# A decoder block in fp32: the first norm's scale row moved from the rows into the raw in-projection weights

## The chip, the cores and the metric

The kernel runs on one core of a Trainium2 chip. A core has TensorE (PE, matmuls; its weight loads are PEld), VectorE (DVE), ScalarE (ACT), GpSimd (POOL) and SyncE (SP, here used only to issue DMAs). They run side by side and are kept in order by semaphores. The metric is the device time of one execution in microseconds; less is better.

## The reference

One layer, 1024 tokens, 1024 channels, all float32:

```
h    = rms_norm(x, norm_mix_pre)              # x * rsqrt(mean(x*x) + eps) * gain
proj = h @ w_in                               # 1024 -> 1792 columns
y    = concat(pool_mixer, conv_mixer, sliding-window attention with sinks)
x    = x + rms_norm(y @ w_o, norm_mix_post)
h    = rms_norm(x, norm_ffn_pre)
up   = causal_dwconv(h @ ffn_w_up) + b        # gate and value, 2816 each
x    = x + rms_norm((silu(gate) * value) @ ffn_w_down, norm_ffn_post)
```

The change concerns the first two lines only. The gain `norm_mix_pre` has one number for each of the 1024 input channels, so (x * r * gain) @ w_in is the same as (x * r) @ (gain * w_in) with the gain on the rows of w_in.

## The kernel before

Tokens lie in eight tiles of 128, channels in eight blocks of 128 (KD), the 1792 in-projection columns in fourteen weight tiles of 128 columns (`IN_ORDER` gives their order). A float32 product is made of three fp32r matmuls: each operand is split into a high part, rounded by ScalarE (`whi`, `hhi`), and a low part, the difference, made by VectorE (`wlo`, `hlo`). TensorE multiplies high by high, high by low and low by high (`product`, lines 1616 to 1618).

The opening works as follows. SP loads x tiles into `xin` (three places, used in turn), the identity matrix, the first gain as eight rows of 128 (`gain_rows`), and again broadcast over all partitions (`gain_a`), and the raw weights into `wraw` (four places, used in turn; a place is loaded again when the low part of its tile is made). For each x tile ScalarE sums the squares (`square_x`), GpSimd makes the reciprocal root (`root`), VectorE writes the normed rows into `hrow_a` (`norm_x`, two places), TensorE turns them so that channels lie on partitions (`turn_x`, eight transposes into two PSUM banks), ScalarE rounds the result to `hhi` (`round_h`) and VectorE makes `hlo` (`low_h`).

Tiles 0 and 1 are normed without the gain, because the broadcast row is not there yet. TensorE transposes `gain_rows` so that the gain lies on channel partitions (line 1684), VectorE copies that to `gain_t`, and multiplies both turned tiles by it in PSUM (`scale_turned`, line 1155). Tiles 2 to 7 are multiplied by root and gain in one instruction (line 1131).

TensorE projects weight tiles 0 and 1 first, two x tiles (a pair) at a time, as the pairs become ready. For pair 0 the products are made pass by pass (`channels_by_pass`, line 1664: eight matmuls for a pass, three passes for a weight tile), with the turns of tiles 2 and 3 between passes; for pairs 1 to 3 in the usual order of `product`. Ahead of the first product TensorE multiplies zeros to keep its clock (`keep_clock`). Weight tiles 2 to 13 follow, with all eight x tiles there; from tile 5 on they are interleaved with the attention's sixteen units (scores, mask, exponentials, `norm_probs`, `turn_probs`, products with the values). Weight tile n is rounded by `round_ring(n)` on ScalarE and `low_ring(n)` on VectorE.

GpSimd's order in this part is: the eight roots, four small DMAs of the pool weights, three small memsets, four DMAs that copy blocks of `w_down` in DRAM, a wait until they are done, two DMAs that add further blocks, a wait, one more, and then the roots of the second norm. Each engine's instructions run in the order in which they are written.

## Time and profile before

| what | value |
|---|---|
| time, median of 3 runs | 950.21 us (949.88 to 950.55) |
| span of the profiled execution, first to last instruction | 948.2 us |
| the median of the runs, beyond that span | 2.0 us |
| TensorE busy | 938.9 us (99%) |
| VectorE busy | 654.7 us (69%) |
| ScalarE busy | 433.5 us (46%) |
| GpSimd busy | 189.4 us (20%) |
| mean granted TensorE clock | 0.999 of 2.4 GHz |

The page of a profile gives each engine's busy time, and the chain of waits: the work that ended last, followed back from the end, each step to what released it. The timeline lists instructions with start and duration; times in it are microseconds from the start of the span.

### The profile page before, as it was taken

Reading aid. Unit: us, or ns where it says so; the run is one execution under the profiler, and the core shown is the slowest. Engines: PE = TensorE matmul, PEld = TensorE weight load, DVE = VectorE, ACT = ScalarE, POOL = GpSimd, SP = SyncE. Lnnn points to the kernel's source line nnn. Section 1 sums busy time; section 2 is a strip of 40 time slices with the busy share of each in tenths; the row PEclk is TensorE's granted clock in tenths of the full one; section 3 lists DMA queues with packets and bytes.
Section 4 is the critical chain, followed back from the end, with each engine's and each line's share of the span. In section 5 each row is a group of like instructions: output and inputs, shape, how many; then the busy total and the mean of one; then the engine's idle time right before and its main releaser. Section 6 shows DMA issues by size and latency. Waiting matters only on the chain.

```text
span 948.2 us, 11487 instructions
## 1 busy us (share of the span) xinstructions
PE 938.9 (99%) x4419; PEld 777.9 (82%) x4419; DVE 654.7 (69%) x710; ACT 433.5 (46%) x648; POOL 189.4 (20%) x182
## 2 busy tenths in 40 slices
PE   8999999999999999999999999999999999999997
PEld 7988887887888888888888888888888888888886
DVE  6645795766655899777877787778776653535668
ACT  5524444444433555445443444444444454335353
POOL 3301000000111424242223333443431100000021
PEclk9999999999999999999999999999999999999999
DMA  6999971005322236486343446554647775677455
GB/s 225 269 328 231 209 145 45 23 23 178 134 89 89 90 97 206 142 184 183 115 141 100 145 112 133 112 143 105 140 91 208 201 235 214 228 267 264 163 171 200
DMA packets 114248, 151.16 MB, mean 159 GB/s; under 512 B 6289, under 2 KB 66193, under 8 KB 114193
## 3 DMA queue, kind: packets, MB, share of 16 engines
q1 hardware_dynamic: 100737, 118.63, 38.5%
q0 software_dynamic: 13456, 31.79, 16.8%
q8 instruction: 35, 0.57, 0.3%
q14 instruction: 20, 0.16, 0.1%
HBM read 113.17 MB, written 60.29 MB: 183 GB/s over the span
## 4 chain that ended last, share of the span: by engine, by line
PE 97%; DVE 1%; DMA 0%; ACT 0%; POOL 0%; issue 0%; DVEq 0%; POOLq 0%; SPq 0%; ACTq 0%
PE ps L1616 30%; PE ps L1618 30%; PE ps L1617 30%; PE ps L1626 1%; PE ps L1751 1%; PE ps L1774 1%; PE ps L1752 1%; PE ps L1760 1%; PE ps L1778 1%; DMA xin<-in_x 0%; DVE hlo L1138 0%; PE ps L1789 0%; DVE ps L1155 0%; PE ps L1664 0%; DVE x2b L1427 0%
## 5 line engine op out<-in xcount | busy, mean ns | idle before, releaser
L1616 PE MATMUL ps<-hhi,whi 128*128 128x512 f32 (+1 forms) x240 | 91.1, 379 | 0.5 <-DVE hlo L1138 0.5
L1618 PE MATMUL ps<-hhi,wlo 128*128 128x512 f32 (+1 forms) x240 | 88.5, 369 | 0.0
L1617 PE MATMUL ps<-hlo,whi 128*128 128x512 f32 (+1 forms) x240 | 88.5, 369 | 0.0
L686 POOL TENSOR_TENSOR w_sums<-wraw 128x1024 f32<-128x1024 f32 x20 | 48.4, 2421 | 185.8 <-DVE w2lo L1373 63.0
L648 POOL TENSOR_SCALAR meansq<-sumsq 128x1 f32<-128x1 f32 x28 | 10.0, 357 | 373.4 <-ACT yg L1042 170.8
L1616 PEld LDWEIGHTS ps<-hhi,whi 128*128 128x128 f32 x240 | 45.3, 189 | 8.0 <-DVE hlo L1138 0.7
L1001 ACT ACTIVATE yg<-ps,par_b 128x1024 f32<-128x1024 f32 x21 | 25.3, 1207 | 57.9 <-DVE ps L1499 57.9
L1618 PEld LDWEIGHTS ps<-hhi,wlo 128*128 128x128 f32 x240 | 45.2, 189 | 7.7
L1617 PEld LDWEIGHTS ps<-hlo,whi 128*128 128x128 f32 x240 | 45.3, 189 | 7.4 <-issue 0.5
L1447 DVE SCALAR_TENSOR_TENSOR yg<-ps,par_a,yg 128x1023 f32<-128x1023 f32 x22 | 28.2, 1282 | 26.9 <-ACT yg L1001 26.9
L1616 PE MATMUL ps<-h2hi,whi 128*128 128x512 f32 x116 | 45.4, 391 | 0.2 <-DVE wraw L1148 0.2
L1618 PE MATMUL ps<-h2hi,wlo 128*128 128x512 f32 x116 | 45.2, 389 | 0.0
L1617 PE MATMUL ps<-h2lo,whi 128*128 128x512 f32 x116 | 45.1, 389 | 0.0
L1461 DVE TENSOR_TENSOR w2lo<-wraw,w2hi 128x1024 fp32r<-128x1024 f32 x23 | 27.8, 1223 | 23.5 <-ACT w2hi L1031 23.1
L1616 PE MATMUL ps<-r_hi,whi 128*128 128x512 f32 x112 | 43.6, 389 | 0.0
L1618 PE MATMUL ps<-r_hi,wlo 128*128 128x512 f32 x112 | 43.6, 389 | 0.0
L1618 PE MATMUL ps<-r_hi,w2lo 128*128 128x512 f32 x112 | 43.6, 389 | 0.0
L1616 PE MATMUL ps<-r_hi,w2hi 128*128 128x512 f32 x112 | 43.6, 389 | 0.0
L1617 PE MATMUL ps<-r_lo,w2hi 128*128 128x512 f32 x112 | 43.6, 389 | 0.0
L1616 PE MATMUL ps<-r_hi,h2hi 128*128 128x512 f32 x112 | 43.6, 389 | 0.0
L1617 PE MATMUL ps<-r_lo,h2hi 128*128 128x512 f32 x112 | 43.6, 389 | 0.0
L1618 PE MATMUL ps<-r_hi,h2lo 128*128 128x512 f32 x112 | 43.6, 389 | 0.0
(261 smaller groups left out, 2709.1 us busy)
## 6 DMA issues: line engine op xcount, KB each, us to landing
wraw<-in_ffn_w_up SPq DMA_DIRECT2D x42, 512.0 KB, 5.2
s_dram<-in_ffn_w_down POOLq DMA_DIRECT2D x6, 2816.0 KB, 28.1
wraw<-r_dram SPq DMA_DIRECT2D x44, 256.0 KB, 3.7
wraw<-s_dram SPq DMA_DIRECT2D x44, 256.0 KB, 4.9
r_dram<-cst SPq DMA_DIRECT2D x33, 256.0 KB, 2.8
wraw<-act_dram SPq DMA_DIRECT2D x33, 256.0 KB, 3.6
wraw<-in_ffn_w_down SPq DMA_DIRECT2D x33, 256.0 KB, 4.6
wraw<-in_w_in SPq DMA_DIRECT2D x14, 512.0 KB, 10.2
```

The costliest lines, as they stand in the source:

```text
L648: pool.tensor_scalar(meansq[:, i:i + 1], sumsq[:, i:i + 1], 1.0 / DM, EPS, ALU.mult, ALU.add).then_inc(ms_ready, 1)
L686: pool.tensor_tensor(w_sums[:, 0:2, :], raw[:, 0:4:3, :], raw[:, 2:3, :].broadcast_to([P, 2, HALF]), ALU.add)\
L1001: act.activation(yg[:, pair % 2, :], banks(4 * (pair % 2)), ACT.Identity, bias=ffn_bias(pair), scale=ffn_tap(2, pair)).then_inc(yg_started, 1)
L1447: finish_step(dve.scalar_tensor_tensor(y[:, 1:], src[:, :SEQ - 1], ffn_tap(1, f), y[:, 1:], ALU.mult, ALU.add))
L1461: dve.tensor_tensor(lo, raw, hi, ALU.subtract).then_inc(d_split, 1)
L1616: pe.matmul(acc, w_hi, x_hi, start=first, stop=False, skip_group_check=looped)
L1617: pe.matmul(acc, w_hi, x_lo, start=False, stop=False, skip_group_check=looped)
L1618: return pe.matmul(acc, w_lo, x_hi, start=False, stop=last, skip_group_check=looped)
L1626: last = pe.transpose(ps[:, b + k // 4, (k % 4) * P:(k % 4 + 1) * P], rows[:, k * P:(k + 1) * P], ident)
L1751: pe.matmul(acc, q, k_hi[:, kv, keys], start=True, stop=False)
L1752: last = pe.matmul(acc, q, k_lo[:, kv, keys], start=False, stop=True)
L1760: last = pe.transpose(ps[:, 6, i * P:(i + 1) * P], s_sb[:, u % 2, i, :], ident)
```

## The change

The gain is no longer multiplied into rows or turned tiles. It is multiplied into the raw weights in `wraw` before these are split. Weight tile 0: the first half on GpSimd (`times_gain`), the second half on VectorE. Weight tile 1: not in place; ScalarE rounds it in eight pieces of 128 columns with the gain as the activation's scale (`round_second`), and VectorE makes the low part in eight pieces (`low_second`). Weight tiles 2 to 13: GpSimd, one instruction each, put between its roots and DMA issues.

Every x tile gets its own place in `xin` and is normed in place, so the loads of x wait for nothing; the squares go to a scratch tile. `hhi` of tile 1 is copied from PSUM by VectorE instead of ScalarE. The broadcast load of the first gain is dropped; the load of the second norm's gain into `gain_a` no longer waits for the rows. The order of SP's loads changes, as do the orders on ScalarE and VectorE for tiles 2 and 3, the places of the turns of tiles 2 and 3 among TensorE's passes, and the split of the keep-clock matmuls.

```
+        gain_t = half_sums
-        xin = alloc(xa, "xin", [P, 3, DM])
-        hrow_a = alloc(xa, "hrow_a", [P, 2, DM])
-        gain_t = alloc(xa, "gain_t", [P, KD])
+        xin = alloc(xa, "xin", [P, NT, DM])
+        squares = alloc(xa, "squares", [P, DM])
...
+        def over_channels(ks):
+            return gain_t[:, ks].rearrange("p (k o) -> p k o", o=1)\
+                .broadcast_to([P, ks.stop - ks.start, P])
...
 SP
             def load_x(t):
-                if t >= 3:
-                    sp.wait_ge(hrow_ready, t - 2)
-                sp.dma_start(xin[:, t % 3, :], x_d[t * P:(t + 1) * P, :])\
-                  .then_inc(xin_in[t % 3], 16)
+                sp.dma_start(xin[:, t, :], x_d[t * P:(t + 1) * P, :]).then_inc(xin_in[t], 16)
             load_x(0)
-            load_x(1)
             sp.dma_start(cst[:, 0:P], consts[:, 0:P]).then_inc(ident_in, 16)
             sp.dma_start(gain_rows[0:KD, :], norm_mix_pre[0].rearrange("(k p) -> k p", p=P))\
               .then_inc(gain_rows_in, 16)
+            load_x(1)
             load_in(0)
             load_x(2)
             load_x(3)
-            sp.dma_start(gain_a[:, :], norm_mix_pre.broadcast_to([P, DM])).then_inc(gain_in, 16)
             load_in(1)
...
-            for n in range(RAW, 6):
+            for n in range(RAW, 7):
                 load_in(n)
-            sp.wait_ge(hrow_ready, NT)
             sp.dma_start(gain_a[:, :], norm_mix_post.broadcast_to([P, DM]))\
               .then_inc(gains_mix_in, 16)
...
 GpSimd
+            def times_gain(n, ks=slice(0, KD)):
+                pool.wait_ge(landed[n % RAW], 16 * (n // RAW + 1))
+                pool.wait_ge(gain_taken, 1)
+                raw = wraw[:, n % RAW, :].rearrange("p (k c) -> p k c", k=KD)[:, ks, :]
+                pool.tensor_tensor(raw, raw, over_channels(ks), ALU.mult).then_inc(gained, 1)
-            for i in range(NT):
+            root(0, 1)
+            root(1, 2)
+            times_gain(0, slice(0, KD // 2))
+            for i in range(2, NT):
                 root(i, i + 1)
+            times_gain(2)
+            times_gain(3)
...          (four DMAs of pool_w)
+            times_gain(4)
+            times_gain(5)
...          (memsets, four DMAs that copy w_down blocks)
+            for n in range(6, 10):
+                times_gain(n)
...          (two DMAs that add blocks)
+            times_gain(10)
+            times_gain(11)
...          (one DMA that adds)
+            times_gain(12)
+            times_gain(13)
 ScalarE
+            def round_second():
+                act.wait_ge(landed[1], 16)
+                act.wait_ge(gain_taken, 1)
+                for k in range(KD):
+                    w = slice(k * P, (k + 1) * P)
+                    last = act.activation(whi[:, 1, w], wraw[:, 1, w], ACT.Copy,
+                                          scale=gain_t[:, k:k + 1])
+                last.then_inc(w_rounded, 1)
             square_x(0)
             square_x(1)
+            round_h(0, hhi)
             round_ring(0)
-            round_h(0, hhi)
-            round_h(1, hhi)
             square_x(2)
             square_x(3)
-            round_ring(1)
-            for t in range(2, NT, 2):
+            round_h(2, hhi)
+            round_second()
+            round_h(3, hhi)
...          (then squares and rounding by pairs, as before)
 VectorE
+            def low_second():
+                dve.wait_ge(w_rounded, 2)
+                for k in range(KD):
+                    w = slice(k * P, (k + 1) * P)
+                    last = dve.scalar_tensor_tensor(wlo[:, 1, w], wraw[:, 1, w], gain_t[:, k:k + 1],
+                                                    whi[:, 1, w], ALU.mult, ALU.subtract)
+                last.then_inc(w_split, 1)
+            dve.wait_ge(gain_turned, 1)
+            dve.tensor_copy(gain_t[:, :], ps[:, 3, 0:KD]).then_inc(gain_taken, 1)
             norm_x(0)
             norm_x(1)
-            dve.wait_ge(gain_turned, 1)
-            finish_step(dve.tensor_copy(gain_t[:, :], ps[:, 3, 0:KD]))
-            scale_turned(0)
-            scale_turned(1)
+            dve.wait_ge(landed[0], 16)
+            dve.wait_ge(gain_taken, 1)
+            raw_late = wraw[:, 0, DM // 2:].rearrange("p (k c) -> p k c", k=KD // 2)
+            dve.tensor_tensor(raw_late, raw_late, over_channels(slice(KD // 2, KD)), ALU.mult)\
+               .then_inc(gained_late, 1)
+            dve.wait_ge(turned, 2)
+            dve.tensor_copy(hhi[:, 1, :, :].rearrange("p k c -> p (k c)"), banks(*turn_banks(1)))\
+               .then_inc(ht_rounded, 1)
             low_ring(0)
             low_h(0, hhi, hlo)
+            norm_x(2)
             low_h(1, hhi, hlo)
-            norm_x(2)
             norm_x(3)
-            low_ring(1)
+            low_h(2, hhi, hlo)
+            low_second()
+            low_h(3, hhi, hlo)
...          (then norms and low parts by pairs, as before)
 TensorE
-                    if n == 1 and i < 2:
-                        turn_x(2 + i)
+                    if n == 0 and i == 2:
+                        turn_x(2)
+                    if n == 1 and i == 0:
+                        turn_x(3)
...
-            keep_clock(8)
+            keep_clock(6)
...          (the gain's transpose)
+            keep_clock(3)
             turn_x(0)
             turn_x(1)
-            keep_clock(4)
+            keep_clock(3)
```

## Rows read from the trace of the kernel before

**Rows 1.** Busy time by stretch: stretch, its length, then each engine's busy time (instructions).

```profile
0.00:12.20 12.20, 9.64 (x41) 7.55 (x41) 5.01 (x7) 6.70 (x9) 2.38 (x11) 1.00 0.82 263
...
21.10:200.00 178.90, 178.78 (x1002) 149.16 (x1003) 117.47 (x193) 78.65 (x209) 15.17 (x22) 1.00 0.67 169
200.00:948.00 748.00, 742.30 (x3314) 613.62 (x3312) 523.93 (x505) 341.66 (x424) 169.29 (x145) 1.00 0.52 155
```

**Rows 2.** Chain of waits up to 21.5 us: start, duration, what.

```profile
1.17 4.40 DMA xin<-in_x
...
7.91 0.49 DVE hrow_a L1126
...
8.77 2.36 DVE ps L1155 x2
...
12.26 2.28 DVE hlo L1138 x2
...
15.86 1.06 PE ps L1626 x8
16.93 0.96 PE ps L1664 x8
...
19.86 1.24 DVE hlo L1138
21.14 0.39 PE ps L1616
```

**Rows 3.** Groups of 0 to 220 us (busy, mean ns), then timeline rows of SP, ScalarE and TensorE.

```profile
L1116 DVE TENSOR_TENSOR wlo<-wraw,whi 128x1024 fp32r<-128x1024 f32 x14 | 17.1, 1220 | 4.4 <-ACT whi L744 4.3
L1126 DVE TENSOR_SCALAR hrow_a<-xin,rstd 128x1024 f32<-128x1024 f32 x2 | 1.5, 754 | 7.2 <-POOL rstd L651 7.2
L1255 DVE TENSOR_TENSOR s_sb<-s_sb,small 128x512 f32<-128x512 f32 x16 | 11.1, 692 | 0.5
...
1.64 0.42 SPq L550 DMA_DIRECT2D cst<-consts_dram  x1
...
8.30 1.06 ACT L744 ACTIVATE whi<-wraw 128x1024 fp32r<-128x1024 f32 x1 [1.55 <-DMA wraw<-in_w_in]
...
15.30 1.06 ACT L744 ACTIVATE whi<-wraw 128x1024 fp32r<-128x1024 f32 x1 [1.03 <-DMA wraw<-in_w_in]
...
12.24 1.21 PE L1664 MATMUL ps<-hhi,whi 128*128 128x256 f32 x8 [0.70 <-ACT hhi L768]
```

**Rows 4.** L686 and L693 alone (duration min/median/max), then timeline of GpSimd and VectorE.

```profile
L686 POOL TENSOR_TENSOR w_sums<-wraw x20: 2384/2391/2702, 341.0 to 689.4; 128x1024 f32<-128x1024 f32 x20
L693 POOL TENSOR_TENSOR w_sums<-w_sums,wraw x20: 1292/1292/1297, 346.9 to 693.5; 128x512 f32<-128x512 f32 x20
...
317.11 4.34 POOL L686 TENSOR_TENSOR w_sums<-w_second 128x1024 f32<-128x1024 f32 x1 [1.45 <-DVE hrow_c L1439]
...
316.89 2.28 DVE L1377 TENSOR_TENSOR r_lo<-wraw,r_hi 128x2048 fp32r<-128x2048 f32 x1
...
324.70 3.38 DVE L1385 SCALAR_TENSOR_TENSOR wraw<-wraw,h2hi 128x2048 f32<-128x2048 f32 x1
```

**Rows 5.** Timeline of ScalarE: one exponential of 128 columns and what follows it.

```profile
80.58 0.39 ACT L825 ACTIVATE s_sb<-s_sb,small 128x128 f32<-128x128 f32 x1
80.87 0.19 ACT L825 ACTIVATION_READ_ACCUMULATOR s_sb<-s_sb,small 128x1 f32 x1
```

**Rows 6.** Timeline: GpSimd's last root, VectorE's low part of weight 2, its first matmul.

```profile
30.76 0.55 POOL L651 TENSOR_TENSOR rstd<-meansq,power 128x1 f32<-128x1 f32 x1
...
40.72 1.23 DVE L1116 TENSOR_TENSOR wlo<-wraw,whi 128x1024 fp32r<-128x1024 f32 x1 [4.34 <-ACT whi L744]
...
42.42 0.48 PE L1616 MATMUL ps<-hhi,whi 128*128 128x512 f32 x1
```

**Rows 7.** Timeline of VectorE and TensorE: unit 2's probabilities normed, and their turn.

```profile
97.14 0.69 DVE L1255 TENSOR_TENSOR s_sb<-s_sb,small 128x512 f32<-128x512 f32 x1
...
98.79 0.62 PE L1760 MATMUL ps<-cst,s_sb 128*128 128x128 f32 x4
```

More of the change, by code:

```diff
@@ L259, in build @@
         gain_turned = sem("gain_pre_on_channel_partitions")
-        scaled = sem("first_turned_rows_scaled")
+        gain_taken = sem("gain_pre_taken_from_psum")
+        gained = sem("weights_times_gain_pre")
+        gained_late = sem("second_half_of_first_weights_times_gain_pre")
         consts_in = sem("consts_in")
@@ L263, in build @@
         pool_w_in = sem("pool_w_in")
-        gain_in = sem("gain_pre_in")
         gains_mix_in = sem("gains_mix_in")
         gain_out_in = sem("gain_out_in")
-        xin_in = [sem(f"xin_in{i}") for i in range(3)]
+        xin_in = [sem(f"xin_in{i}") for i in range(NT)]
         xres_in = sem("xres_in")
@@ L573, in _ @@
             sp.dma_start(sinks[:, :], attn_sinks.broadcast_to([P, NH])).then_inc(params_in, 16)
-            for n in range(RAW, 6):
+            for n in range(RAW, 7):
                 load_in(n)
-            sp.wait_ge(hrow_ready, NT)
             sp.dma_start(gain_a[:, :], norm_mix_post.broadcast_to([P, DM]))\
               .then_inc(gains_mix_in, 16)
-            for n in range(6, NIN):
+            for n in range(7, NIN):
                 load_in(n)
@@ L742, in round_weight @@
                 n = base + RAW * q
-                act.wait_ge(landed[base % RAW], 16 * (base // RAW + 1 + q))
+                if n == 0:
+                    act.wait_ge(gained, 1)
+                    act.wait_ge(gained_late, 1)
+                elif n < NIN:
+                    act.wait_ge(gained, n)
+                else:
+                    act.wait_ge(landed[base % RAW], 16 * (base // RAW + 1 + q))
                 act.activation(hi[:, slot, :], wraw[:, base % RAW, :], ACT.Copy)\
@@ L751, in round_ring @@
                 round_weight(n, 0, whi, r % SPLIT)
+            def round_second():
[6 more added lines that the diff above has]
+                last.then_inc(w_rounded, 1)
             def square_x(t):
-                act.wait_ge(xin_in[t % 3], 16 * (t // 3 + 1))
-                if t >= 2:
-                    act.wait_ge(turned, t - 1)
-                act.activation(hrow_a[:, t % 2, :], xin[:, t % 3, :], ACT.Square,
+                act.wait_ge(xin_in[t], 16)
+                if t:
+                    act.wait_ge(squared, t)
+                act.activation(squares[:, :], xin[:, t, :], ACT.Square,
                                accum_out=sumsq[:, t:t + 1]).then_inc(squared, 1)
             def round_h(i, hi):
-                if i < 2:
-                    act.wait_ge(scaled, i + 1)
                 act.wait_ge(turned, i + 1)
@@ L772, in _ @@
             square_x(1)
+            round_h(0, hhi)
             round_ring(0)
-            round_h(0, hhi)
-            round_h(1, hhi)
             square_x(2)
             square_x(3)
-            round_ring(1)
-            for t in range(2, NT, 2):
+            round_h(2, hhi)
+            round_second()
+            round_h(3, hhi)
+            for t in range(4, NT, 2):
+                square_x(t)
+                square_x(t + 1)
                 round_h(t, hhi)
                 round_h(t + 1, hhi)
-                if t + 2 < NT:
-                    square_x(t + 2)
-                    square_x(t + 3)
             def take(m):
@@ L1632, in turn_x @@
                     pe.wait_ge(ht_split, t - 1)
-                turn(t, hrow_a[:, t % 2, :])
+                turn(t, xin[:, t, :])
             def channels(acc_bank, slot, hi, lo, tiles, ks=range(KD)):
```

28 lines of the change are left out of this document (8 added, 20 removed).

## The prediction

> **What bounds the kernel now.** I read the busy time by stretch first. From 21.1 us to 200 us TensorE is busy 178.78 of 178.90 us, and from 200 us to the end 742.3 of 748; the first 12.2 us hold 2.56 us without TensorE work [rows 1]. DMA is busy about two thirds of the time behind 21.1 us, ScalarE and VectorE less. So TensorE's own work is the bound, the change alters none of the products, and it can win only what lies ahead of the first ordinary matmul of tile pair 1, which starts at 21.14 us. Everything behind follows that start, since TensorE has no gap in which a later start could be made up. The change can lose in two places: in this opening, and wherever GpSimd's new work makes VectorE late for TensorE further on.
>
> The chain of waits tells what the opening is made of [rows 2]: x tile 1 lands at 5.57; its squares and root, and its norm at 7.91; both turned tiles times the gain on VectorE, 2.36 us; wlo; two hlo to 14.54; then passes of eight matmuls on TensorE with the turns of tiles 2 (15.86) and 3 between them, a last hlo of tile 3 (19.86), and pair 1 at 21.14. From 8.77 to 14.54 VectorE alone sets the pace.
>
> **The change, part by part.** Durations are in [rows 3]; consecutive VectorE and ScalarE instructions overlap by about 0.1 us.
>
> *Removed.* The two products L1155 (2.36 us on the chain). The product into rows of tiles 2 to 7 becomes the plain scaling that tiles 0 and 1 have now, 0.75 us (L1126). The gain broadcast and the waits of the x loads leave SP's early queue; that hides nothing from the bound, because from x tile 1 on no transfer stands in the chain. Weight tile 1 comes earlier than now, when ScalarE waited for it until 15.30; that matters only if ScalarE is free for it, and below it is not.
>
> *x tile 1 later.* The identity (64 KB) and the gain rows (4 KB) now go ahead of it. Tile 1 took 4.40 us from issue to landing behind tile 0's 512 KB [rows 2]; 68 KB at the 263 GB/s of this stretch [rows 1] is 0.26 us. If the later issue counts instead, it is two issues of 0.42 us, 0.9 with what lies between. I take the bytes, since tile 0 keeps the DMA engines at work meanwhile: tile 1 lands at 5.8, and the norm starts between 8.05 and 8.15 instead of 7.91; I go on with 8.05. With the norm's 0.75 us and the turn's 1.1 (L1626 in rows 2) the turned tile is there at 9.95.
>
> *The gain into weight tile 0.* Weight tile 0 lands at about 8.3 as before (ScalarE's rounding waited for it until 8.30), as the bytes ahead of it are the same. Then half of it is multiplied on GpSimd and half on VectorE. GpSimd: 1.29 us for 128x512 (L693). VectorE: 0.69 us (L1255, the same shape with a broadcast small operand). They are meant to run side by side. The trace speaks against that [rows 4]: GpSimd's L686 takes 2.39 us as a rule and 4.34 us when VectorE's L1377, with both inputs in SBUF, was under way (316.89 to 319.17); 319.17 plus 2.39 is 321.56, and it ended at 321.45. The other way round, VectorE's L1385 took 3.38 us, 1.1 more than L1377 took for as many elements, while GpSimd was at work on the last sum of the same tile. One waits for the other to end. The same at 8 us: the norm of tile 1 runs 8.05 to 8.8, GpSimd's half 8.8 to 10.1, VectorE's half 10.1 to 10.8, ScalarE's rounding of whi 10.8 to 11.85. Without the waiting GpSimd would be done at 9.6, and the first product would start at 11.3 (behind the copy of the turned tile 1, 10.0 to 11.25), 0.65 us earlier than with it.
>
> The Trainium skill has this rule ("SBUF — State Buffer", Who interferes with whom): a VectorE instruction with two SBUF inputs contends with a GpSimd instruction that reads SBUF, and the one that starts first keeps the port to its end. The rows above agree. By the rule the opening ends 0.65 us later than if both halves ran in parallel; the sum takes the rows' value, which is the same.
>
> *hhi of tile 1 on VectorE.* 1.2 us like L1116, behind VectorE's half of the gain: 10.75 to 11.95. First product at 11.95 instead of 12.24 [rows 3]. Then VectorE does wlo (11.9 to 13.1), hlo of tile 0 (to 14.25), the norm of tile 2 (to 14.9), hlo of tile 1 (to 16.05). Before, the two hlo ended at 14.54.
>
> *Tiles 2 and 3 and weight tile 1.* The turn of tile 2 starts at 14.95 instead of 15.86; with 1.1 us for the turn ScalarE rounds tile 2 from 16.05 to 17.1. Now comes the dear part: weight tile 1 is rounded in eight pieces of 128 columns with a per-partition scale, where one instruction of 1.06 us did it. The nearest row is L825, the same shape: 0.39 us, and 0.29 us from one start to the next instruction's [rows 5]. Eight make 2.4 us (bounds: 8 x 0.2 = 1.6, the 0.19 us of an instruction with one element, and 8 x 0.39 = 3.1). ScalarE: 17.0 to 19.4. Before, whi of tile 1 was ready at 16.36. VectorE's wlo in eight pieces: between 128x512 (0.69) and 128x1024 (1.22) an element costs 1.03 ns and an instruction 0.16, so a piece is 0.30, with the overlap 0.21, together 1.7 us instead of 1.22: 19.4 to 21.1. hlo of tile 3 follows, 21.05 to 22.3. TensorE: third pass of weight 0 from 16.1, turn of tile 3 to 18.0, wait, weight 1's three passes 19.4 to 22.3 (0.96 us each, the pass of 16.93 in rows 2). Pair 1 starts at 22.35 instead of 21.14: **plus 1.2 us**. Bounds: pieces at 1.6 us and no waiting between GpSimd and VectorE give 20.9 (minus 0.2); the longer pieces and x tile 1 at 0.9 us late give 23.8 (plus 2.7).
>
> *Keep-clock matmuls* move (6, 3, 3 instead of 8 and 4) and cost nothing: they lie in waits, and the later three end at about 11.2, ahead of 11.95.
>
> *GpSimd's twelve other tiles.* Twelve of 128x1024 at 2.39 us are 28.7 us on an engine that is busy 15.2 of 178.9 us [rows 1], so none is on the path by itself. A tile's place is loaded again three weight tiles ahead of its use, 144 matmuls at a mean of 0.18 us or 26 us, and one product takes 2.39. Moved behind them are GpSimd's own DMA issues: the copies of the w_down blocks start 8 to 10 us later (four products), their sums too; they are read in the last stage only, and the transfers of weights 7 to 13 beside them stay as crowded as now. What counts is whom a product blocks. First, GpSimd's last root was done at 31.31 [rows 6], now 1.2 later; the norm of tile 7 (0.75), weights 2 and 3 (4.8) and four DMA issues (0.4 to 0.6 each) put weights 4 and 5 at about 40.3 to 45. VectorE's low part of weight 2, before at 40.72, ends 0.47 us ahead of its user. Shifted by 1.2 it comes at 41.9, is held until 42.7 and ends at 43.9 where TensorE wants it at 43.6: **plus 0.3** (bounds 0 and 2.0). Second, in the attention stage the normed probabilities of unit 2 are ready 0.96 us ahead of TensorE's turn of them [rows 7], and in eight others of the sixteen units 1.1 to 1.4 us; a product that starts just before a VectorE instruction with two SBUF inputs holds it up to 2.39 us. Weights 9 to 13 come here as they land, about one in two units. Most overlaps stay within the spare time; I take one that goes 0.2 us beyond it: **plus 0.2** (bounds 0 and 5 x 1.4 = 7).
>
> *SP.* The x tiles and weights 1 to 3 are issued one behind the other (12 issues of 0.42 us, by 7 us); the load of the second norm's gain goes behind weight 6 and is wanted behind the attention. Nothing.
>
> Sum: 1.2 + 0.3 + 0.2 = 1.7 us on a span of 948.2. The median of the runs is 950.21, 2.0 above the span; I add the sum to it: **951.9 us**. A measurement tells about 0.2% (1.9 us) from no change, so this is within it, on the slow side.
>
> **The rivals.**
> 1. *The opening is nearly even.* If the pieces are cheap or the two halves do run side by side, pair 1 starts between 20.9 and 21.7: 950.0 to 950.9. For: an activation of 128 columns needs little of its 0.39 us for the columns. Against: [rows 4, 5].
> 2. *Slower: GpSimd's products hold VectorE in the attention stage.* Place: weights 9 to 13, on the chain from a unit's scores to its normed probabilities. Spare is about 1.1 us; a full block is 2.39. It decides the sign as soon as blocks beyond the spare add up to 0.5 us more than I took. With three of five hit at a mean 0.65 over the spare it is 2.0 instead of 0.2: 953.7. For: VectorE is busy 117 of 179 us there, and low parts and probabilities all have two SBUF inputs. Against: the tiles land at times that TensorE's order doesn't choose, and some units have 3 us to spare.
> 3. *The clock.* TensorE now waits about 1.4 us ahead of weight 1 and 0.9 us ahead of tile 2's turn. Granted clock stays 1.00 over 2.56 us of waits now [rows 1]. Should it fall to 1.2 GHz for 3 us of work, they take 3 more: 954.9.
> 4. *Faster: the whole of L1155 is won.* If ScalarE's and VectorE's pieces hide behind TensorE, pair 1 starts at 21.14 - 2.36 + 0.15 = 18.9, minus 2.2: 948.0. It needs weight 1's high part by 16.5, before the turn of tile 3 is over; ScalarE would have to take the pieces ahead of tile 2, and its order doesn't.
>
> **How the numbers follow.** Forecast 0.45 (own range 950.5 to 953.0, two thirds of it within 0.2%), rival 1 0.20, rival 2 0.22, rival 3 0.05, rival 4 0.08. Faster by over 0.2% (below 948.3): 0.08. Slower (above 952.1): 0.15 + 0.22 + 0.05 = 0.42. Within: 0.50. The range leaves out rival 4, rival 3 and the far end of rival 2: 949.6 to 954.2.
>
> **What the profile after will show.** First product near 11.95; GpSimd's half of weight 0 at 1.3 us but starting to count only when the norm of tile 1 is over, or VectorE's half far longer than 0.69 us; eight activations over about 2.4 us from 17; TensorE idle ahead of weight 1's first pass; pair 1 at 22.35. VectorE's low part of weight 2 longer than 1.22 us. In the attention stage idle TensorE time where there was none, each with a GpSimd product beside it. I am wrong if pair 1 starts before 20.9 or after 23.8, or if GpSimd and VectorE show their usual durations side by side.

## The result, and the profile after

The changed kernel takes **960.00 us** (median of 4 runs, 959.37 to 961.88) against 950.22 us (949.88 to 950.55): ratio 1.0106, interval 1.0094 to 1.0118. It is slower by 9.8 us. The prediction was 951.9 us with a range of 949.6 to 954.2: wrong, and by far more than its range. The profiled executions stand 10.3 us apart (958.5 against 948.2 us).

Busy time by stretch of the changed kernel, read as in [rows 1] (stretch, length, busy time of TensorE, weight loads, VectorE, ScalarE, GpSimd, granted clock, DMA share, GB/s):

```profile
0.00:12.20 12.20, 7.77 (x31) 6.16 (x32) 3.04 (x4) 4.68 (x7) 3.17 (x12) 0.95 0.83 267
12.20:21.10 8.90, 8.10 (x52) 7.13 (x50) 7.17 (x7) 5.38 (x11) 1.63 (x4) 0.87 1.08 357
21.10:200.00 178.90, 172.82 (x968) 144.07 (x969) 123.73 (x189) 77.73 (x202) 37.27 (x34) 1.00 0.63 157
200.00:958.00 758.00, 752.57 (x3371) 621.93 (x3369) 530.18 (x518) 345.93 (x437) 169.78 (x145) 1.00 0.52 153
```

Between 21.1 and 200 us TensorE had 0.12 us without work before; now it has 6.08. Behind 200 us it idles 5.4 us of 758 against 5.7 of 748, so nothing is lost there. Of the 6.08, 1.18 us belong to a wait of the opening (ahead of 22.28). Two places carry the loss: the opening and the attention stage.

**The opening.** The chain of waits of the changed kernel up to the passes of weight 1:

```profile
2.05 5.63 DMA xin<-in_x
...
7.70 1.16 ACT squares L794 x2
...
9.79 1.53 DVE xin L1169
...
11.37 1.98 PE ps L1663 x8
...
13.37 1.23 DVE hhi L1198
14.60 1.13 DVE wlo L1151
15.73 1.14 DVE hlo L1175
16.86 0.67 DVE xin L1169
...
17.67 1.08 PE ps L1663 x8
...
22.28 3.35 PE ps L1703 x24
```

Timeline rows of the same kernel that belong to it (start, duration, instruction, idle time before it and what ended it):

```profile
9.73 1.04 POOL L660 TENSOR_TENSOR wraw<-wraw,half_sums 128x512 f32<-128x512 f32 x1
...
11.37 1.97 PE L1663 MATMUL ps<-cst,xin 128*128 128x128 f32 x8 [3.17 <-DVE xin L1169]
...
25.54 0.39 PE L1653 MATMUL ps<-hhi,whi 128*128 128x256 f32 x1
```

And two microseconds of the turn of tile 1, as stretches (the third figure from the right is the granted clock):

```profile
12.00:13.00 1.00, 1.00 (x7) 1.00 (x6) 0.00 (x0) 0.99 (x2) 0.00 (x0) 0.50 1.07 356
13.00:14.00 1.00, 1.00 (x5) 0.82 (x4) 0.63 (x1) 1.00 (x3) 0.00 (x0) 0.50 1.03 401
```

These rows show four things. x tile 1 lands at 7.68 us, not at 5.57 [rows 2]. Its norm takes 1.53 us instead of 0.75: GpSimd's half of weight 0 started at 9.73, 0.06 us ahead of it. TensorE has nothing to do for 3.17 us and comes back at the lower of its two clock levels (0.50, that is 1.2 GHz), so that the turn takes 1.97 us instead of 1.1. Pair 1 starts at 25.54 instead of 21.14: **4.4 us**, where the prediction had 1.2.

**From there to 44 us.** The norm of the last x tile is held in the same way by the gain of weight 2, and TensorE waits 0.42 us for it. These are the timeline rows of GpSimd's root of that tile, its products, VectorE's norm, and TensorE's turn:

```profile
34.40 0.55 POOL L652 TENSOR_TENSOR rstd<-meansq,power 128x1 f32<-128x1 f32 x1
34.91 4.20 POOL L660 TENSOR_TENSOR wraw<-wraw,half_sums 128x1024 f32<-128x1024 f32 x2
...
34.98 2.38 DVE L1169 TENSOR_SCALAR xin<-xin,rstd 128x1024 f32<-128x1024 f32 x1 [0.71 <-POOL rstd L652]
...
37.50 1.06 PE L1663 MATMUL ps<-cst,xin 128*128 128x128 f32 x8 [0.42 <-DVE xin L1169]
```

**The attention stage.** One stretch of the timeline shows it: rows of VectorE, of GpSimd, and TensorE's turn of the probabilities:

```profile
94.02 2.14 DVE L1292 TENSOR_TENSOR s_sb<-s_sb,small 128x512 f32<-128x512 f32 x1
96.08 0.73 DVE L1276 COPY_PREDICATED s_sb<-cst,ps 128x512 f32<-128x512 uint32 x1
96.85 0.69 DVE L1280 TENSOR_REDUCE small<-s_sb 128x4 f32<-128x512 f32 x1
97.57 3.00 DVE L1281 SCALAR_TENSOR_TENSOR small<-small,neg_sinks 128x4 f32<-128x4 f32 x1
...
91.85 3.75 POOL L660 TENSOR_TENSOR wraw<-wraw,half_sums 128x1024 f32<-128x1024 f32 x2 [4.06 <-DMA wraw<-in_w_in]
95.55 1.54 POOL L685 DMA_DIRECT2D s_dram<-in_ffn_w_down  x1
96.45 2.16 POOL L687 DMA_DIRECT2D s_dram<-in_ffn_w_down  x1
97.33 3.20 POOL L660 TENSOR_TENSOR wraw<-wraw,half_sums 128x1024 f32<-128x1024 f32 x1
...
96.21 0.66 PE L1800 MATMUL ps<-cst,s_sb 128*128 128x128 f32 x4 [1.03 <-DVE s_sb L1292]
```

The probabilities' product with two inputs in SBUF, 0.69 us before [rows 3], takes 2.14 while GpSimd works on weights 8 and 9. An instruction of 128x4, 0.16 to 0.17 us elsewhere, takes 3.00. The two between them take their usual time; they have one SBUF input and start beside the DMA issues alone. (In e12, below, the same two start inside a product, at 87.92 and 88.70, and take 0.74 and 0.69 us as well. One SBUF input is no safeguard for every instruction, though: the norm of the rows has one, beside a number for each partition, and it was held above.) TensorE's idle time behind 44 us is 4.5 us, in waits of 1.03, 0.74, 1.20 and 1.38 us that VectorE ends and some smaller ones; its granted clock is 1.00 there throughout. GpSimd's root of the second norm, a mark behind the attention, comes at 244.44 instead of 234.15. So 10.3 us = 4.4 (pair 1) + 0.3 (from there to the first matmul of weight 2, at 47.15 instead of 42.42) + 5.6. The 1.1 us by which the 5.6 exceed the idle time come in steps of 0.1 to 0.3 us around the waits; what makes them stays open.

### The profile page after: what moved, and what is told of

It reads as the page before. It is cut to its first block, busy times and chain, and to the rows that moved or that the text cites. A ratio compares the mean times of both kernels' runs of the same rounds, so it can differ in the third digit from the quotient of the medians.

```text
span 958.5 us, 11525 instructions
## 1 busy us (share of the span) xinstructions
PE 941.3 (98%) x4419; PEld 779.3 (81%) x4419; DVE 664.1 (69%) x717; ACT 433.7 (45%) x654; POOL 211.9 (22%) x195
## 4 chain that ended last, share of the span: by engine, by line
PE 89%; DVE 7%; ACT 2%; issue 1%; DMA 1%; POOL 0%; SPq 0%; DVEq 0%; POOLq 0%; ACTq 0%
PE ps L1653 28%; PE ps L1655 28%; PE ps L1654 28%; PE ps L1663 1%; DVE wlo L1151 1%; DVE pool_d L1331 1%; DVE s_sb L1292 1%; DVE s_sb L1276 1%; DMA xin<-in_x 1%; DVE small L1280 1%; ACT s_sb L860 1%; PE ps L1814 1%; PE ps L1791 1%; DVE q_parts L1244 1%; DVE xin L1169 0%
## 5 line engine op out<-in xcount | busy, mean ns | idle before, releaser
L660 POOL TENSOR_TENSOR wraw<-wraw,half_sums 128x1024 f32<-128x1024 f32 (+1 forms) x13 | 26.1, 2021 | 80.5 <-DMA wraw<-in_w_in 80.5
L1654 PE MATMUL ps<-r_lo,whi 128*128 128x512 f32 x112 | 43.6, 389 | 0.0
## 6 DMA issues: line engine op xcount, KB each, us to landing
wraw<-in_w_in SPq DMA_DIRECT2D x14, 512.0 KB, 13.8
```

The costliest lines, as they stand in the source:

```text
L660: pool.tensor_tensor(raw, raw, over_channels(ks), ALU.mult).then_inc(gained, 1)
L1654: pe.matmul(acc, w_hi, x_lo, start=False, stop=False, skip_group_check=looped)
```

## The experiments

Results, all in microseconds; "pair 1" is the start of the first ordinary matmul in the profiled execution (21.14 before, 25.54 after). The runs e3, e5, e6, e10 and e11 leave part of the gain out, so they compute something else and only tell what the rest costs. Each run has one trace. With x tile 1 issued second it landed between 5.57 and 5.86 us in seven of them (before, e1, e5, e6, e9, e10, e11); in its later place it landed at 6.82, 7.07, 7.23, 7.68 and 8.09 (e12, e3, e4, after, e2). Differences of a microsecond between single traces of the later place can therefore be scatter. The kernel before had medians of 950.30 (e1 to e4), 950.36 (e5 to e8) and 950.19 (e9 to e12) beside them.

| run | median (range) | ratio to before, interval | pair 1 |
|---|---|---|---|
| e1 x tile 1 second | 961.39 (959.94–963.17) | 1.0118 (1.0103–1.0133) | 22.56 |
| e2 weight 0 all on VectorE | 961.55 (956.85–962.91) | 1.0110 (1.0084–1.0136) | 24.64 |
| e3 no gain in weights 2 to 13 | 952.92 (952.29–953.57) | 1.0028 (1.0018–1.0038) | 24.06 |
| e4 before, x tile 1 late | 951.28 (950.78–952.29) | 1.0011 (1.0001–1.0020) | 22.57 |
| e5 e1 and e3 together | 951.35 (950.90–951.98) | 1.0011 (1.0001–1.0020) | 23.27 |
| e6 e1 without weight 10's gain | 958.09 (957.25–959.54) | 1.0083 (1.0069–1.0096) | 22.62 |
| e7 e4, x tile 1 transferred alone | 951.17 (950.69–951.77) | 1.0009 (1.0000–1.0018) | 22.25 |
| e8 before, gain spread by TensorE | 952.32 (950.49–952.89) | 1.0014 (1.0005–1.0023) | 22.06 |
| e9 e1, weights 2 to 13 by pieces | 955.28 (954.38–957.14) | 1.0050 (1.0034–1.0065) | 23.78 |
| e10 e5, weight 0 all on VectorE | 950.92 (950.27–951.61) | 1.0007 (0.9999–1.0016) | 22.13 |
| e11 e5, x loads wait again | 951.31 (951.14–951.66) | 1.0013 (1.0004–1.0021) | 22.78 |
| e12 after, clock kept | 957.37 (956.41–961.77) | 1.0084 (1.0064–1.0104) | 24.30 |

**e1: x tile 1 second again.** In the changed kernel:

```
             load_x(0)
+            load_x(1)
             sp.dma_start(cst[:, 0:P], consts[:, 0:P])...
             sp.dma_start(gain_rows[0:KD, :], ...)...
-            load_x(1)
```

> The changed kernel with one difference: SP issues x tile 1 directly behind x tile 0 again, ahead of the identity and the gain rows. Theory A (the place in SP's order makes x tile 1 late, and that lateness makes TensorE wait long enough to lose its clock): tile 1 lands near 5.6 us instead of 7.7, TensorE's granted clock stays at 1.00 in the opening, the first product starts at 12 to 12.5 us instead of 14.9, pair 1 at about 22.5 instead of 25.5, and the time is 956.5 to 957.5 us. Rival B (tile 1 is late because the loads of x and of the weights, now issued without waits, share the DMA engines): it still lands after 7 us and the time stays at 959.5 or more.

The opening came out nearly as the prediction had drawn it: the norm started at 8.10, the halves of weight 0 ran one behind the other, the clock stayed at 1.00, pair 1 started at 22.56 (predicted 22.35). That is 3.0 us earlier than after, and yet the time didn't fall: Theory A had the opening right and the time (956.5 to 957.5) wrong. The attention stage lost what the opening had won. Timeline rows of e1 on VectorE, GpSimd and TensorE:

```profile
92.02 5.10 DVE L1292 TENSOR_TENSOR s_sb<-s_sb,small 128x512 f32<-128x512 f32 x1
...
91.58 1.54 POOL L685 DMA_DIRECT2D s_dram<-in_ffn_w_down  x1
92.48 2.16 POOL L687 DMA_DIRECT2D s_dram<-in_ffn_w_down  x1
93.36 3.20 POOL L660 TENSOR_TENSOR wraw<-wraw,half_sums 128x1024 f32<-128x1024 f32 x1
...
97.17 1.12 PE L1800 MATMUL ps<-cst,s_sb 128*128 128x128 f32 x4 [4.94 <-DVE s_sb L1292]
```

And its stretches from inside that wait on:

```profile
95.00:100.00 5.00, 2.83 (x9) 2.44 (x10) 4.90 (x7) 1.84 (x7) 1.56 (x1) 0.50 1.07 178
100.00:105.00 5.00, 5.00 (x20) 3.93 (x19) 4.69 (x7) 0.66 (x5) 0.00 (x0) 0.86 1.12 204
```

One instruction of 0.69 us was held for 5.10, TensorE waited 4.94, and its clock fell to 0.50 within that wait and stayed there until 101.4. From 97.2 to 101.4 TensorE worked at half speed, which is some 2.1 us lost (an estimate from these two times). Where the products land against VectorE's work decides, and here they met a worse place than in the changed kernel.

**e2: the gain of weight 0 on VectorE alone**, the GpSimd half taken out of the changed kernel:

```
-            times_gain(0, slice(0, KD // 2))
-            raw_late = wraw[:, 0, DM // 2:]...          (four channel blocks)
+            raw_late = wraw[:, 0, :]...                 (all eight)
```

> The changed kernel with one difference: all of weight tile 0 is multiplied by the gain on VectorE, in one instruction of 128x1024, and nothing of it on GpSimd. Theory A (GpSimd's half took the shared port first and held the norm of x tile 1 from 0.75 to 1.52 us): the norm of tile 1 takes 0.75 us, its turn starts 0.75 us earlier and the time falls by 0.7 to 1.2 us (less waiting, perhaps less of the low clock), to about 959. Rival (the two engines' halves do save time together, since the product on VectorE alone is 1.22 instead of 0.68 us): the first product starts no earlier, and the time is 960 or more.

The norm of tile 1 took its 0.75 us again (it started at 10.21, as x tile 1 landed at 8.09), and pair 1 started at 24.64, 0.9 earlier than after. The clock fell to 0.50 all the same, at 11.9, behind a wait of 2.50 us. The time tells nothing: its runs lie 6 us apart, and the profiled one has a wait of 5.2 us in the attention stage. The hold of the norm is shown by the trace, its price in the time is not.

**e3: no gain in weights 2 to 13**, all twelve GpSimd products out of the changed kernel:

```
-            times_gain(2)
...
-            times_gain(13)
```

> The changed kernel without the gain in weight tiles 2 to 13 (this part of the computation is left out; the opening with weight tiles 0 and 1 is unchanged): GpSimd has none of its twelve products and ScalarE rounds as the tiles land. Theory A (GpSimd's products hold VectorE's instructions with two SBUF inputs, and that is all of the loss between 44 and 200 us): TensorE has no waits there, and the time is 5.0 to 5.6 us below the changed kernel, about 954.6. Rival (the loss there comes from the new order of loads and of the w_down copies, or from late weights): at least 2 us of waits stay in that stretch, and the time is above 956.5.

Windows of e3, same columns:

```profile
25.00:40.00 15.00, 15.00 (x130) 15.00 (x129) 6.98 (x7) 6.07 (x8) 5.42 (x13) 1.00 0.11 29
40.00:80.00 40.00, 40.00 (x207) 34.25 (x207) 16.61 (x17) 13.16 (x14) 2.74 (x4) 1.00 0.98 312
...
80.00:200.00 120.00, 120.00 (x653) 96.85 (x652) 88.80 (x163) 57.93 (x184) 4.55 (x3) 1.00 0.59 122
```

TensorE has no gap left behind 25 us, and the time falls by 7.1 us (960.00 to 952.92). In the profiled executions 1.5 of that stand in the opening, where no product of these differs (x tile 1 landed at 7.07 instead of 7.68), so the twelve products are worth some 5.6 to 7.1 us. The remaining 2.6 us over before are the opening. The rival (late weights, the new order of loads) is out: the orders are the same here and no wait is left. There is a second sign. In the traces without the twelve products (before, e3, e5, e9) no VectorE instruction between 21 and 210 us takes over 0.12 us more than the shortest of its kind; in the changed kernel seven do, by 11.7 us in all, and each overlaps a product.

**e4: the kernel before, with x tile 1 issued behind the identity and the gain rows**, as in the change:

```
             load_x(0)
-            load_x(1)
             sp.dma_start(cst[:, 0:P], consts[:, 0:P])...
             sp.dma_start(gain_rows[0:KD, :], ...)...
+            load_x(1)
```

> The kernel before with one difference: the identity and the gain rows are issued ahead of x tile 1, as in the changed kernel; x tile 3 still waits for the first normed row. Theory A (place in the order alone): tile 1 lands at 7.0 to 7.7 us instead of 5.57, the opening is later by 1.5 to 3 us, time 951.7 to 953.2. Rival B (only together with the x loads that no longer wait): tile 1 lands by 6.2, time within 0.7 us of 950.2. The estimate of the prediction was 5.8 us.

The time rose by 1.0 us, less than the 1.5 that Theory A gave at the least, though the landing is the one it gave. x tile 1 was issued 0.88 us later (2.05 against 1.17) and landed 1.66 us later (7.23 against 5.57).

**e7: why it lands so late.** e4, with SP waiting for x tile 1 before it issues weight 0:

```
             load_x(1)
+            sp.wait_ge(xin_in[1], 16)
             load_in(0)
```

> The kernel before with the identity and the gain rows issued ahead of x tile 1, and SP waiting until tile 1 has landed before it issues weight tile 0. Theory A (tile 1 lands 1.7 to 2.1 us late because its packets share the DMA engines with those of weight tile 0 and x tile 2, once it has lost its lead): it lands at 5.5 to 6.1 us here, while weight tile 0 comes late and sets the opening (time about 951.5 to 953). Rival (the small transfers ahead of it, the identity in 512 byte pieces and the gain rows, cost it that time themselves): it lands at 7.0 or later.

x tile 1 from issue to landing in the chain of waits of e4:

```profile
2.05 5.18 DMA xin<-in_x
```

The same of e7:

```profile
2.05 4.27 DMA xin<-in_x
```

Alone it takes 4.27 us and lands at 6.32. So of the 1.66 us, 0.9 goes with the traffic issued behind it and 0.8 with the two small loads ahead. That is a split of single traces; the 6.32 lies below all five landings of the later place (6.82 to 8.09), so the direction is safe and the sizes are rough. In the kernel before it took 4.40 [rows 2], hardly longer than alone. That it was well under way there when the next loads came is my explanation, which no run tests. Neither expectation of e7 held alone.

**e5: x tile 1 second and no gain in weights 2 to 13** (the edits of e1 and e3).

> The changed kernel with x tile 1 issued directly behind tile 0 and without the gain in weight tiles 2 to 13 (that part of the computation is left out): GpSimd has only its half of weight tile 0. What is left of the change is its opening. Theory A (the losses add up: late x tile 1 with the low clock about 3 us, GpSimd's later products the rest): pair 1 starts near 22.6 us as in the run with tile 1 second, no TensorE waits behind it, time 951.5 to 952.0 us, which is what the prediction gave for the opening alone (plus 1.2, and 0.3). Rival (another loss stays behind 21 us): 953 or more.

951.35 us, where 951.5 to 952.0 were expected, and no wait of TensorE behind the opening; pair 1 came at 23.27 instead of 22.6. Against e1, which differs by the twelve products alone, that is 10.0 us. With the pair after and e3 (7.1) this gives their price twice, and shows that it depends on where they land. Counted from pair 1 on in the traces, the prices are 8.8 and 6.2 us. The runs with tile 1 second show another thing. In e1, e5, e9 and e11 weight tile 0 landed between 8.79 and 10.01, it heads the chain of waits, and pair 1 starts 13.8 us behind it each time. In e6 and e10 it landed at 8.70 and 8.23, and VectorE's own chain was about as late (13.9 us). So once tile 1 is early, the transfer of weight tile 0 can set the opening; the prediction had it at 8.3 and off the chain.

**e6: e1 without weight 10's gain alone**, the product that stands behind two DMA issues.

```
-            times_gain(10)
```

> The changed kernel with x tile 1 second and without the product of weight tile 10 alone (its gain is left out), the one that stands behind GpSimd's two issues of the w_down sums and held a 0.69 us instruction of VectorE for 5.10 us. Theory A (the large loss is that pile: product 8 and 9, two DMA issues, product 10 back to back, and the low clock that follows the long wait): the wait of 4.9 us near 92 us falls under 1.5 us, the clock stays at 1.00 and the time falls by 4 to 6 us, from about 961 to 955 to 957. Rival (each of the twelve products costs about the same, 0.5 to 0.8 us): the time falls by less than 1.5 us.

3.3 us less than e1, a third of the 10.0, so the other eleven cost twice as much together, if the prices add up. Theory A (4 to 6 us) gave too much and the rival (under 1.5) too little. The wait near 92 us fell to 2.06 us, not under 1.5, and the clock still fell to 0.50 there (94.8 to 98.2). Timeline of e6, VectorE and GpSimd:

```profile
90.92 0.98 DVE L1287 TENSOR_TENSOR small<-small 128x4 f32<-128x4 f32 x1 [1.22 <-ACT small L862]
...
92.15 2.14 DVE L1291 TENSOR_TENSOR s_sb<-s_sb,small 128x512 f32<-128x512 f32 x1
...
95.70 0.16 DVE L1280 SCALAR_TENSOR_TENSOR small<-small,neg_sinks 128x4 f32<-128x4 f32 x1
...
93.68 1.54 POOL L685 DMA_DIRECT2D s_dram<-in_ffn_w_down  x1
94.58 2.16 POOL L687 DMA_DIRECT2D s_dram<-in_ffn_w_down  x1
```

Products 8 and 9 still hold two instructions (0.98 and 2.14 us). The DMA issues alone hold none: 0.16 us at 95.70, in their midst, and the traces without products show the same. It takes a product behind them to hold VectorE, and then, in e1, from 92.02, before the product's own record begins at 93.36.

**e9: the gain of weights 2 to 13 without GpSimd**, by eight pieces each on ScalarE and VectorE, as weight 1 has it (with e1's order of loads; the whole computation is done):

```
+                if 2 <= n < NIN:           (round_ring; low_ring has the same)
+                    for k in range(KD):
+                        w = slice(k * P, (k + 1) * P)
+                        last = act.activation(hi[:, slot, w], wraw[:, base % RAW, w], ACT.Copy,
+                                              scale=gain_t[:, k:k + 1])
```

> The changed kernel with x tile 1 second and GpSimd's products of weight tiles 2 to 13 replaced: these tiles take the gain as tile 1 does, in eight scaled pieces on ScalarE and eight on VectorE (the whole computation is there). Each tile costs ScalarE 2.4 instead of 1.06 us and VectorE 2.2 instead of 1.22, in the order in which they worked before, and nothing holds the shared port. Theory A (what the twelve products cost, 10.0 us in the versions with tile 1 second, is the port and not the work): 951.4 to 953 us, waits of TensorE behind 21 us under 1.5 us in all. Rival (VectorE and ScalarE have no room in the attention stage for any more work): above 955.

955.28 us. With the products off GpSimd no VectorE instruction is held between 21 and 210 us, and 6.1 of e1's 10.0 us come back; the other 3.9 (over e5) are the price of the pieces. The time is what the rival gave (above 955), but the want of room is not in the attention stage: of 2.4 us that TensorE idles between 44 and 210 us, 1.8 stand ahead of weight 2 (first row below) and 0.6 in the attention stage. The clock was at 0.50 from 47.6 to 51.0, behind that wait. The profiled run is the slowest of the four (957.14). Timeline of e9, where TensorE waits for a low part in pieces:

```profile
46.82 0.47 PE L1656 MATMUL ps<-hhi,whi 128*128 128x512 f32 x1 [1.82 <-DVE wlo L1149]
...
52.32 2.19 DVE L1149 SCALAR_TENSOR_TENSOR wlo<-wraw,half_sums,whi 128x128 fp32r<-128x128 f32 x8
```

**e10: e5 with the gain of weight 0 on VectorE alone** (the edit of e2).

> As the run with x tile 1 second and no gain in tiles 2 to 13, and with all of weight tile 0 multiplied on VectorE (one 128x1024 product) instead of half on each engine. If the two halves run one after the other (1.29 and 0.69 us, 2.0 together with the wait), VectorE alone with 1.22 us brings whi of tile 0 some 0.3 to 0.6 us earlier, and the time falls from 951.35 to 950.7 to 951.1. If they run side by side as the change has it, it rises by 0.5.

950.92 us, 0.4 less than e5, or 0.3 when each is compared with the kernel before beside it. Timeline rows, of e10's VectorE and of e5's GpSimd:

```profile
8.70 1.22 DVE L1181 TENSOR_TENSOR wraw<-wraw,half_sums 128x1024 f32<-128x1024 f32 x1
...
9.57 1.54 POOL L660 TENSOR_TENSOR wraw<-wraw,half_sums 128x512 f32<-128x512 f32 x1 [1.61 <-DMA wraw<-in_w_in]
```

One product of 128x1024 takes 1.22 us. The two halves take 1.58 together: VectorE's from 9.53 to 10.22, GpSimd's from 9.57 to 11.11, where 1.04 is its usual time. ScalarE starts weight 0 at 9.95 instead of 11.15, but most of that is not the edit: weight tile 0 landed at 8.23 here and at 9.51 in e5. It is the nearest that any variant of the change came to the kernel before (950.19 beside it), and it leaves out most of the gain.

**e11: e5 with the x loads waiting for their place again.**

```
             def load_x(t):
+                if t >= 3:
+                    sp.wait_ge(hrow_ready, t - 2)
```

> As the run with x tile 1 second and no gain in tiles 2 to 13, and x tiles 3 to 7 wait for the normed rows again before they are issued, as in the kernel before. Theory A (loads that no longer wait share the DMA engines with weight tile 0, which landed at 8.8 to 9.5 us instead of 8.2): it lands at 8.3 or earlier, the first product starts 0.4 to 1.0 us earlier, 950.6 to 951.0 us. Rival (weight tile 0 lands as late, or ScalarE's eight pieces of weight tile 1 set the pace anyway): no change from 951.35 by more than 0.3.

951.31 against 951.35: x tiles loaded without a wait cost nothing that the time shows. Weight tile 0 landed at 9.01, no earlier than in e1 (8.79), so the rival holds.

**e12: the changed kernel with TensorE kept at work between the turns of tiles 0 and 1.**

```
             turn_x(0)
+            keep_clock(6)
             turn_x(1)
```

> The changed kernel as it is, with six more matmuls of zeros between the turns of x tiles 0 and 1, where TensorE waits 3.2 us and its granted clock then falls to 0.50 from 11 to 14.4 us. Theory A (the low clock costs in the opening): granted clock stays at 1.00, the turn of tile 1 takes 1.09 instead of 1.97 us, and pair 1 starts 0.9 to 1.5 us earlier than 25.54. Rival (the clock costs nothing, as VectorE or ScalarE come last anyway): pair 1 within 0.3 us. The time itself, 960.0, can move by more either way, since GpSimd's later products fall on other instructions of VectorE.

The turn takes 1.04 us instead of 1.97, the granted clock is 1.00 throughout the opening, pair 1 starts 1.24 us earlier. The median is 2.6 us lower, but its runs spread over 5.4 us. Nor is the 1.24 the price of the clock: tile 1 landed at 6.82 here, 0.86 earlier than after, and the added matmuls kept the turn until 11.06 where the norm was over at 10.46. Timeline of e12, TensorE and then VectorE's norm of tile 1:

```profile
11.06 1.04 PE L1663 MATMUL ps<-cst,xin 128*128 128x128 f32 x8
11.93 1.46 PE L1716 MATMUL ps<-pool_mat 128*128 128x256 f32 x6
13.41 1.21 PE L1703 MATMUL ps<-hhi,whi 128*128 128x256 f32 x8
...
8.94 1.52 DVE L1169 TENSOR_SCALAR xin<-xin,rstd 128x1024 f32<-128x1024 f32 x1 [1.81 <-POOL rstd L652]
```

The cleaner pair is after and e3, whose opening is the same. In e3 tile 1 landed at 7.07, TensorE waited 1.85 us, and the clock did not fall:

```profile
10.77 1.09 PE L1651 MATMUL ps<-cst,xin 128*128 128x128 f32 x8 [1.85 <-DVE xin L1157]
```

Its pair 1 starts 1.48 us earlier than after: 0.61 of landing and 0.87 of the clock. Counted from the landing of tile 1, pair 1 comes 17.0 us later in e3, 17.5 in e12 and 17.9 after, so the added matmuls won back 0.4 of the 0.9 us.

**e8: another way to be rid of L1155.** In the kernel before, TensorE spreads the gain row over all partitions in PSUM (two calls with a row of ones, four matmuls in the trace), and the norms of tiles 0 and 1 multiply by root and gain in one instruction; row and identity come through ScalarE's DMA queue. Ahead of the turns zeros are multiplied six times instead of eight, four of them ahead of the spread.

```
+            act.dma_start(gain_rows[0:1, :], norm_mix_pre).then_inc(gain_rows_in, 16)
+                last = pe.matmul(ps[:, 1 + 2 * b, :], ones[0:1, :],
+                                 gain_rows[0:1, b * HALF:(b + 1) * HALF], start=True, stop=True)
+                    dve.scalar_tensor_tensor(hrow_a[:, t, :]..., xin[:, t, :]...,
+                                             rstd[:, t:t + 1], ps[:, 1:4:2, :], ...)
-            scale_turned(0)
-            scale_turned(1)
```

> A version of the kernel before that takes the removed step out in another way: ScalarE's queue issues the gain row (4 KB, one partition) and the identity at the very start, TensorE spreads the row over all partitions by two matmuls with a row of ones into two free PSUM banks, and VectorE norms x tiles 0 and 1 times root and gain in one instruction each (1.28 instead of 0.75 us), like the other tiles; the two products of 2.36 us on the chain are gone, nothing is added to GpSimd. If VectorE sets the pace between 8.8 and 14.5 us as the chain says: pair 1 starts 0.8 to 1.2 us earlier than 21.14, time 949.0 to 949.5 us. Rival (the turns then wait for the longer norms and the squares of tile 2 for ScalarE, so nothing moves): 950.0 to 950.5.

No gain: neither 949.0 to 949.5 nor the rival's 950.0 to 950.5. The spread takes 2.33 us (4.97 to 7.30), so the norms start at 7.41, and pair 1 comes at 22.06, later than before. The granted clock also fell here, to 0.50 from 9.1 to 12.5 us, and the two turns took 3.36 us, where they took 1.09 each in the kernel before:

```profile
8.75 3.36 PE L1618 MATMUL ps<-cst,hrow_a 128*128 128x128 f32 x16 [0.39 <-DVE hrow_a L1126]
```

What this way would give at full clock no run tells. Its 11 runs fall into two groups, near 950.6 (mean granted clock 0.997 to 0.998, the profiled one among them) and near 952.7 (0.999); why the group with the higher clock is slower I can't say.

## Why the prediction was wrong, by its own steps

The prediction called itself wrong if pair 1 started after 23.8; it started at 25.54. Of its sum, 1.2 + 0.3 + 0.2 us, the first term measured 4.4 and the last 5.6.

**x tile 1 later: failed, size.** The step took the bytes ahead of it (0.26 us, bound 0.9). It landed 2.1 us later (7.68 against 5.57); e4 shows 1.66 in the kernel before, and e7 splits that roughly in half: what lay behind the load in the queue counted as much as what lay ahead. Of a transfer's 4.40 us [rows 2] I had asked only what precedes it.

**The norm goes first, then GpSimd's half: failed.** That the two can't overlap was right, but the order was given by tile 1's arrival, which I had at 5.8. Weight 0 was there by the time GpSimd had made the root of tile 1, and the product stands directly behind that root on the same engine, while the norm waits for it across engines. So the product starts first (9.73 against 9.79; at 34.91 against 34.98 for the last tile; by 0.06 or 0.07 us in all eight such meetings of the traces), and the norm is held by 0.8 and 1.6 us. The prediction's own rule, that the one that starts first makes the other wait [rows 4], would have told this, had I asked who starts first for *every* product behind a root. The Trainium skill says so too ("SBUF — State Buffer", Who interferes with whom): issue order decides who is blocked. The trace agrees (1.53 us for a norm of 0.75). One record does not fit it: in e1 VectorE's instruction started at 92.02 by its record, 1.3 us ahead of the product's, and was held all the same.

**Keep-clock matmuls cost nothing: failed.** The later norm left TensorE 3.17 us without work, the clock fell to 0.50, and the turn took 0.9 us more; after against e3 gives the same 0.9 us for pair 1. The 2.56 us of waits that the prediction took as proof of a safe clock were several, of 1.26 us at most. Rival 3 named the mechanism with a chance of 0.05 and put it behind the first product.

Together: tile 1 lands 1.9 later than predicted and its norm starts 1.7 later, is held 0.8, its turn slower by 0.9, so that it is turned at 13.35 instead of 9.95. VectorE was to round it at 10.75, 0.8 behind the turn; that slack is used up, and it starts 2.6 late (13.37). The first product comes 3.0 later than predicted (14.91 against 11.95), pair 1 3.2 later.

**Weight tile 0 at 8.3: failed, without effect here.** It landed at 9.37, still ahead of GpSimd's start at 9.73. With tile 1 early it can set the opening (see e5). That the same bytes ahead give the same landing is not borne out (8.23 to 10.01 in the traces of the changed opening), nor is it that no transfer stands in the chain behind tile 1.

**Pieces: right on ScalarE, 0.5 us short on VectorE.** ScalarE's eight took 2.43 us (predicted 2.4), VectorE's eight 2.19 (predicted 1.7), TensorE waited 1.47 us ahead of weight 1's passes. With x tile 1 early (e1) the whole opening is 0.2 us from the prediction. That closeness is partly luck: the same opening gave 22.62 to 23.78 in e5, e6, e9 and e11, with the landing of weight tile 0.

**Low part of weight 2, plus 0.3: right size, wrong place.** VectorE's low part took its 1.23 us (45.45), but the norm of tile 7 was held by weight 2's product, 0.42 us of TensorE's time.

**The attention stage, plus 0.2: this is the step that failed most.** The mechanism was rival 2's, to which I gave 0.22 and 2.0 us. It cost 5.6 us in the profiled execution; the two pairs of medians, which hold differences of the opening too, give 7.1 and 10.0. The bound in the sum, 5 x 1.4 = 7, would nearly have held; the value chosen, and rival 2's price, did not. Three things were missed. I took one hold per product, of 2.39 us at most; a single product was cheaper (1.90 us), but two products come back to back when their weights have landed (8 and 9 in 3.75 us), and a product behind two DMA issues held one instruction for 5.10 us. I priced the one instruction that a product meets, while a unit's chain has four with two SBUF inputs, down to 128x4, and each can be held (0.17 to 3.00 us). And a long wait can lower the clock: in e1 a turn took 1.12 us instead of 0.60. In the profiled execution of the changed kernel it didn't, so its 5.6 us are holds alone; its other executions (mean clock 0.993 to 0.995 against 0.997) may have had it.

**SP: nothing, right** (e11). **GpSimd not on the path by itself: right**; TensorE never waited for a product directly.

**Open.** Why a product queued behind DMA issues held VectorE before its own record begins; the 1.1 us of the attention stage beyond TensorE's idle time; and the two groups of e8. No variant beat the kernel before.

## What to carry to other kernels

Before putting work on GpSimd because it is idle, list VectorE's instructions with two SBUF inputs on the critical chain, and the scalings of whole rows (the norm here was held with one), and ask for each GpSimd instruction which of them it can hold: the price is the hold, not the instruction, and GpSimd work in a row (products and the DMA issues between them) counts as one block. A GpSimd instruction directly behind the one that releases VectorE went first in all eight cases here; put it elsewhere. A load at the head of the chain should keep its place in the queue. For each new wait of TensorE ask what a lower clock behind it would cost (0.9 us in this opening), and whether the work put in to keep it delays what it is to save (0.5 us here).

## What the runs showed of the hardware that I had not expected

- A VectorE instruction of 128x4 (0.16 us) took 3.00 us, and one of 128x512 (0.69 us) 5.10, beside GpSimd's work. The norm of a row tile, with one SBUF input, took 1.52 and 2.38 instead of 0.75 us. DMA issues of GpSimd alone held nothing (0.16 us in their midst in e6; 0.69 for the 128x512 at 119.14 in the kernel before, beside the issue at 117.97).
- GpSimd's product with a broadcast operand took 1.90 us for 128x1024 alone, less than the sum of two tensors (2.39 [rows 4]).
- A 512 KB load issued 0.88 us later landed 1.66 us later in the kernel before; with nothing issued behind it until it was there, 0.75 (single traces; the later place scattered from 6.82 to 8.09).
- Eight activations of 128 columns with a per-partition scale: 2.43 us; one of 1024: 1.06.
